# Spreading the decays' running sums with short products on four row groups of TensorE

## The chip, the cores and the metric

The kernel runs on one core of one Trainium2 chip, in one launch. The metric is the device time of an execution in microseconds (us); the runs are compared by their median.

## The reference, cut to what matters

The model is two stacked blocks over 256 tokens of width 1024, each of depth 2. The first block mixes three branches per layer: a state-space branch (ssd), latent attention, and a gated delta rule (gdn). The change concerns ssd and gdn, and there the decays. Both branches work in chunks and need, for every head, the difference of running sums of a decay `A` between every pair of positions of a chunk:

```
A_cum = jnp.cumsum(A, axis=-1)                                    # ssd: 16 heads
L = jnp.exp(jnp.where(tril, A_cum[..., :, None] - A_cum[..., None, :], -jnp.inf))
...
g = jnp.cumsum(chunks(g), axis=-1)                                # gdn: 8 heads
decay = jnp.exp(jnp.where(incl, g[..., :, None] - g[..., None, :], -jnp.inf))
```

On the chip a chunk is 128 positions for both branches (two chunks, c = 0 and 1), and position is the partition. So `A_cum[s]` down the partitions is a column, easily had, while `A_cum[t]` along the free axis has to be the same in all 128 partitions: a row that is spread to all partitions.

## The kernel before

**Engines and order.** Each engine runs its own program, written as generators; a hand-written order (`order1`) interleaves them turn by turn, the same order on every engine. A turn is either a step of a stage (gdn, ssd) or a "fill": one step of a large dense projection, 256 output columns, 48 matmuls in fp32r (lines 942 to 944, three per contraction tile, weights split in a high and a low half). ScalarE makes the high halves of the weights (line 1544), VectorE the low ones (line 2192; GpSimd for some), two chunks ahead. The weights come by 1 MB transfers into a ring of three units, each started by SyncE when TensorE is done with a unit.

**Banks.** PSUM has eight banks, and `open` hands them out strictly in turn: each call takes the oldest one and puts it at the end of the list (only the banks of a running power sum are held longer). TensorE waits in `open` until the previous user of that bank is emptied, that is, until the engines that read it have said so. So an `open` waits for the user that stands eight `open`s before it.

**The running sums.** `small` computes the decays `dA` [128 positions, 2 chunks, 24 heads] (0 to 15 ssd, 16 to 23 gdn) and by a product with the triangle `tri` the column form `cum` (lines 1085 to 1087, copied by ScalarE at 1807 and 1808). The row form is computed where it is needed, once per head and chunk: a column of `dA` broadcast to 128 columns is the stationary operand, `tri` the moving one, 128 rows of contraction (lines 1116 and 1247). All of these are fp32 products, and each shows as two records in the trace.

**gdn, four steps** `(c, g)` = (0,0), (0,1), (1,0), (1,1), each followed by a fill (`z`, `z`, `gate_g`, `gate_g`). TensorE opens bank `gd_b`, makes four row forms, opens `gd_qk` and makes four products of q and k (1122, 1123), then does the fill. ScalarE takes exp of `gd_b` (1836), waits for VectorE's clamp, takes exp of that (1839), makes high halves, and copies the fill's bank out through Silu or Sigmoid (1632), which is another table of functions. VectorE subtracts the column form from `gd_b` (2493), which empties it, clamps (2496), and makes the masked products (2498 to 2503). After the four steps come transposes (867) of what VectorE made.

**ssd, eight steps** `(c, q)`, four heads each: TensorE opens `sd_l` and makes four row forms; for the second chunk ScalarE takes exp of it (1925); VectorE subtracts and clamps (2627, 2631), which empties it, and ScalarE takes exp (1928). Fills stand behind six of the eight steps (`lat`, `lat`, none, `wgo`, `wgo`, `wgo`, none, `wgo`). `wgo` reads the gdn result, split by ScalarE (1579) and VectorE (2249). Then come the products of the stage (1256, 1269), the latter after VectorE's 2657.

Both layers of the first block run this; the second block does not use it.

Of the kernel before, what the change touches and what calls it, by code (L numbers as in the profile page):

```python
# [5 lines left out]
F32 = mybir.dt.float32  # L6
# [4 lines left out]
ACT = mybir.ActivationFunctionType  # L11
# [58 lines left out]
def bc(ap, shape):  # L70
    return ap.to_broadcast(shape)
# [89 lines left out]
class Shared:  # L161
# [18 lines left out]
    def up(self, who, name, tag):  # L180
        now = self.now
        assert not tag or (name, tag) not in now.after, (name, tag)
        assert now.owner.setdefault(name, who) == who, name
        now.n[name] = now.n.get(name, 0) + 1
        now.after[name, tag] = now.n[name]
        return self.sem(name), 1
# [4 lines left out]
    def at(self, name, tag):  # L191
        return self.sem(name), 1 if self.known is None else self.known.after[name, tag]
# [16 lines left out]
    def bank(self, tag):  # L209
        return self.ps[:, (self.known or self.now).bank_of[tag], :]  # L210
# [151 lines left out]
    def memory(self):  # L362
        nc = self.nc
        self.ps = self.ctx.enter_context(nc.psum_tensor("ps", [128, 8, 512], F32))
        self.home = (nc.sbuf_base + 31) // 32 * 32
        self.slab = self.sb("slab", [128, ARENA])
        self.ring = self.sb("ring", [128, (2 * RAW + HI) * SLOT])
        self.lows = [self.rounded(ARENA + 2 * i * SLOT, 2 * SLOT) for i in range(RAW)]
        self.highs = [self.rounded(ARENA + 2 * (RAW + i) * SLOT, 2 * SLOT) for i in range(HI // 2)]
        x2 = self.sb("x2", [128, 8, 512])  # L370
        self.x2 = x2[:, :, :]
        self.x = x2[:, :, 0:256]
        cst = self.sb("cst", [128, len(CONSTS), 128])
        self.cst = cst[:, :, :]
        self.C = {k: cst[:, i, :] for i, k in enumerate(CONSTS)}
        u = CONSTS.index("u0")
        self.upper = [cst[:, u + 2 * x:u + 2 * x + 2, :].rearrange("p n (a b) -> p (n a) b", b=16) for x in range(2)]
        o1, n1 = offsets(VEC1)
        o2, n2 = offsets(VEC2)
        v1, v2 = self.sb("v1", [128, 2, n1]), self.sb("v2", [128, 2, n2])  # L380
        self.v1, self.v2 = v1[:, :, :], v2[:, :, :]
        self.V1 = [{k: v1[:, l, a:b] for k, (a, b) in o1.items()} for l in range(2)]
        self.V2 = [{k: v2[:, l, a:b] for k, (a, b) in o2.items()} for l in range(2)]
        posi = self.sb("posi", [128, T], I32)
        trig = self.sb("trig", [128, 2 * T])
        self.posi, self.trig, self.cos, self.sin = posi[:, :], trig[:, :], trig[:, 0:T], trig[:, T:2 * T]
        qg8 = self.sb("qg8", [128, 1])
        self.qg8 = qg8[:, :]
        eps = self.sb("eps", [128, 1])
        self.eps = eps[:, :]  # L390
        zero = self.sb("zero", [128, 1])
        self.zero = zero[:, :]
        cvec, silc = self.sb("cvec", [128, 8, 2]), self.sb("silc", [128, 8, 50])
        self.cvec, self.silc = cvec[:, :, :], silc[:, :, :]
        row = self.sb("row", [128, 256])
        self.row = row[:, :]
        mods = self.sb("mods", [128, 2, 48, 2])
        self.mods = [mods[:, l, :, :] for l in range(2)]
        self.block1_memory()
        self.block2_memory()  # L400

# [448 lines left out]
class TensorE(Engine):  # L850
# [13 lines left out]
    def turn(self, P, aps):  # L864
# [2 lines left out]
            i = self.e.transpose(P[:, j * 128:j * 128 + 128], ap, self.K.C["ident"])  # L867
        return i

    def weights(self, chunk):  # L870

        K, p = self.K, self.K.take(chunk)
        if K.known is None:
            return p, K.lows[0][:, 0:K.wide_of(chunk)], K.lows[0][:, 0:K.wide_of(chunk)]
        if p in K.by_pool:
            self.wait_ge(*self.at("w_lo_g" if K.by_pool[p] else "w_lo_v", p))
            return p, K.high(p), K.low(p)
        self.wait_ge(K.raw_sem(p), K.raw_value(p))
        return p, K.raw(p), None
# [195 lines left out]
    def small(self, L):  # L1075
        K, up, at, e = self.K, self.up, self.at, self.e
        yield from self.rows(K.jobs1[L]["wsm"])
        yield
        yield
        yield  # L1080
        P = self.open("cum", L)
        self.wait_ge(K.sem("constants"), 16)
        self.wait_ge(*at("sm_v", "dA", L))
        dA = K.dA
        for c in range(2):
            self.mm(P[:, 24 * c:24 * c + 24], K.C["tri"], dA[:, c, :], True, True)
        self.mm(P[:, 64:88], K.C["ones"], dA[:, 0, :], True, True).then_inc(*up("sm_p", "cum", L))
        yield

    def qk(self, L):  # L1090
# [5 lines left out]
    def gdn(self, L):  # L1096
# [12 lines left out]
                self.turn(P, [vT[:, 4 * g + h, cs] for h in range(4)]).then_inc(*up("gd_p", "vt", L, c, g))  # L1109
        yield  # L1110

        for c, g in CG:
            cs = slice(c * 128, c * 128 + 128)
            P = self.open("gd_b", L, c, g)
            for j in range(4):
                i = mm(bank(P, j), bc(K.dA[:, c, 16 + 4 * g + j:17 + 4 * g + j], [128, 128]), K.C["tri"], True, True)
            i.then_inc(*up("gd_p", "b", L, c, g))
            P = self.open("gd_qk", L, c, g)
            self.wait_ge(*at("qk_v", "q", L))
            for j in range(2):  # L1120
                h = 2 * g + j
                mm(bank(P, 2 * j), kT[:, h, cs], kT[:, h, cs], True, True)
                i = mm(bank(P, 2 * j + 1), kT[:, h, cs], qT[:, h, cs], True, True)
            i.then_inc(*up("gd_p", "qk", L, c, g))
            yield
# [111 lines left out]
    def ssd(self, L):  # L1237
        K, up, at, e, mm = self.K, self.up, self.at, self.e, self.mm
        acc = K.s_acc

        yield

        for c in range(2):
            for q in range(4):
                P = self.open("sd_l", L, c, q)
                for j in range(4):
                    i = mm(P[:, j * 128:j * 128 + 128], bc(K.dA[:, c, 4 * q + j:4 * q + j + 1], [128, 128]), K.C["tri"], True, True)
                i.then_inc(*up("sd_p", "l", L, c, q))
                yield

        for c in range(2):
            cs = slice(c * 128, c * 128 + 128)
            P = self.open("sd_cb", L, c)
            self.wait_ge(*at("cv_s", "silu", ("xbc", L), 11))
            for g in range(2):
                i = mm(P[:, g * 128:g * 128 + 128], acc[:, 8 + g, cs], acc[:, 10 + g, cs], True, True)
            i.then_inc(*up("sd_p", "cb", L, c))
            for g in range(2):
                P = self.open("sd_x", L, c, g)
                self.turn(P, [acc[:, 4 * g + j, cs] for j in range(4)]).then_inc(*up("sd_p", "x", L, c, g))  # L1260
        yield

        P = self.open("sd_bt", L)
        self.turn(P, [acc[:, 8 + g, 0:128] for g in range(2)]).then_inc(*up("sd_p", "bt", L))
        for g in range(2):
            P = self.open("sd_h", L, g)
            self.wait_ge(*at("sd_v", "Xs", L))
            self.wait_ge(*at("sd_s", "bt", L))
            mm(P, K.Bt[:, g, :], K.Xs[:, 512 * g:512 * g + 512], True, True).then_inc(*up("sd_p", "h", L, g))
        yield  # L1270

        half = [slice(64 * j, 64 * j + 64) for j in range(2)]
        for c in range(2):
            for g in range(2):
                P = self.open("sd_y", L, c, g)
                self.wait_ge(*at("sd_v", "LC", L, c, 2 * g + 1))
                self.wait_ge(*at("sd_v", "Xd", L, c, g))
                for i in range(4):
                    for j in range(2):
                        h = 8 * g + 2 * i + j  # L1280
                        m = mm(P[half[j], 128 * i:128 * i + 128], K.Xd[:, c, 64 * h:64 * h + 64], K.L2[:, c, h, :], True, True)
                m.then_inc(*up("sd_p", "y", L, c, g))
            if c == 0:
                for g in range(2):
                    P = self.open("sd_off", L, g)
                    self.wait_ge(*at("sd_s", "h", L, g))
                    for i in range(4):
                        m = mm(P[:, 128 * i:128 * i + 128], K.Hs[:, g, 128 * i:128 * i + 128], acc[:, 10 + g, 128:256], True, True)
                    m.then_inc(*up("sd_p", "off", L, g))
            yield  # L1290

        self.stats(("so", L), 8, 4, T, K.C["ones"], K.sq)
        yield
# [237 lines left out]
class ScalarE(Engine):  # L1531
# [253 lines left out]
    def small(self, L):  # L1785
# [21 lines left out]
        self.act(K.cum, P[:, 0:48].rearrange("p (a b) -> p a b", a=2), ACT.Copy).then_inc(*up("sm_s", "cum", L))  # L1807
        self.act(K.tot, P[:, 64:88], ACT.Copy).then_inc(*up("sm_s", "tot", L))
        self.emptied("sm_s", "cum", L)
        yield  # L1810

    def qk(self, L):
# [1547 lines left out]
```

## Time and profile before

| | |
|---|---|
| median of 3 runs | 2505.55 us (2504.55 to 2507.82) |
| profiled execution | 2503.62 us, its span 2501.8 us |
| TensorE (PE) | busy 97% of the span, 20550 matmul records |
| VectorE (DVE) / ScalarE (ACT) / GpSimd (POOL) | busy 58% / 50% / 12% |
| mean granted TensorE clock | 0.988 of full |

The first block's layers lie at about 17 to 675 us and 675 to 1330 us; gdn's four steps run at 94 to 124 us and 753 to 783 us, ssd's eight at 258 to 301 us and 917 to 960 us. A row's start is counted from the span's start. Matmuls overlap, so the price of one in a stream is the distance between starts and not its duration. PE is TensorE's matmul, PEld its weight load, SP SyncE.

### The profile page before, as it was taken

To read this page: it belongs to the slowest core of one execution; us is meant where nothing else is said; L and a number is where in the kernel's file an instruction comes from. 1 tells how busy PE (TensorE), PEld (TensorE's weight loads), DVE (VectorE), ACT (ScalarE), POOL (GpSimd) and SP (SyncE) were. 2 spreads that over 40 slices of the span, in tenths; PEclk is the share of its full clock that TensorE was granted. 3 is DMA by queue.
4 is the path that set the end of the run, shared out by engine and by line. 5 is a ranking of instruction groups with operands and counts; after the bars stand their busy time and mean duration, and the time that the engine had idled before them with its cause. 6 is when DMAs were issued, how large, how long until landed. Compare 5 with 4: busy or idle time off the path is not lost.

```text
span 2501.8 us, 46658 instructions
## 1 busy us (share of the span) xinstructions
PE 2419.7 (97%) x20550; PEld 2251.4 (90%) x20550; DVE 1452.0 (58%) x2202; ACT 1244.5 (50%) x1832; POOL 301.2 (12%) x171
## 2 busy tenths in 40 slices
PE   6999999999999999999999999999999999998999
PEld 6999998999999999989999886887789997778999
DVE  5773776665457457756655347643335555776554
ACT  5745654554466375555544367532223444344442
POOL 4213000000141220001000004200000001331000
PEclk9999999999999999999999999999999999999999
DMA  4344444555444343545553235333325542213554
GB/s 174 136 151 169 149 160 164 196 183 192 157 169 152 138 167 135 186 163 193 188 189 129 101 136 202 127 115 130 104 99 198 199 145 99 86 69 135 185 186 169
DMA packets 56058, 383.01 MB, mean 153 GB/s; under 512 B 6064, under 2 KB 9776, under 8 KB 10288
## 3 DMA queue, kind: packets, MB, share of 16 engines
q1 hardware_dynamic: 55104, 375.90, 42.0%
q10 hardware_dynamic: 752, 4.13, 0.5%
q8 instruction: 162, 2.65, 0.4%
q14 instruction: 40, 0.33, 0.0%
HBM read 377.91 MB, written 1.05 MB: 151 GB/s over the span
## 4 chain that ended last, share of the span: by engine, by line
PE 80%; DVE 10%; ACT 6%; DMA 2%; issue 1%; POOL 0%; DVEq 0%; ACTq 0%; POOLq 0%
PE ps L942 20%; PE ps L944 20%; PE ps L943 20%; DVE r L2192 3%; ACT r L1544 2%; PE ps L1071 1%; PE ps L1023 1%; PE ps L1025 1%; PE ps L1024 1%; PE ps L980 1%; PE ps L901 1%; PE ps L981 1%; PE ps L982 1%; PE ps L867 1%; PE ps L1169 1%
## 5 line engine op out<-in xcount | busy, mean ns | idle before, releaser
L942 PE MATMUL ps<-r,r 128*128 128x256 f32 (+1 forms) x4464 | 1329.0, 298 | 8.7 <-DVE slab L2990 4.9
L943 PE MATMUL ps<-r,r 128*128 128x256 f32 (+1 forms) x4464 | 1314.1, 294 | 0.0
L944 PE MATMUL ps<-r,r 128*128 128x256 f32 (+1 forms) x4464 | 1313.2, 294 | 0.0
L2192 DVE TENSOR_TENSOR r<-ring,r 128x1024 fp32r<-128x1024 f32 (+2 forms) x558 | 678.0, 1249 | 515.8 <-ACT r L1544 515.5
L942 PEld LDWEIGHTS ps<-r,r 128*128 128x128 f32 x4464 | 843.8, 189 | 43.0 <-issue 5.8
L944 PEld LDWEIGHTS ps<-r,r 128*128 128x128 f32 x4464 | 843.2, 189 | 25.0
L943 PEld LDWEIGHTS ps<-r,r 128*128 128x128 f32 x4464 | 843.8, 189 | 24.2 <-issue 0.5
L1544 ACT ACTIVATE r<-ring 128x1024 fp32r<-128x1024 f32 (+1 forms) x614 | 612.7, 1038 | 280.4 <-DMA ring<-in_fo 63.7
L3114 POOL TENSOR_TENSOR slab<-slab 128x512 f32<-128x512 f32 (+1 forms) x20 | 28.7, 1433 | 1238.5 <-ACT slab L1660 1218.3
L3066 POOL TENSOR_TENSOR r<-ring,r 128x1024 fp32r<-128x1024 f32 x56 | 133.2, 2398 | 233.0 <-ACT r L1544 223.1
L2281 DVE SCALAR_TENSOR_TENSOR slab<-ps,v,slab 128x255 f32<-128x255 f32 (+1 forms) x168 | 67.8, 474 | 76.6 <-ACT slab L1612 76.6
L980 PE MATMUL ps<-r,r 128*128 128x256 f32 x288 | 86.9, 302 | 13.4 <-DVE r L2368 7.6
L1023 PE MATMUL ps<-r,r 128*128 128x256 f32 (+2 forms) x304 | 89.3, 294 | 0.4 <-DVE r L2192 0.4
L1025 PE MATMUL ps<-r,r 128*128 128x256 f32 (+2 forms) x304 | 87.4, 288 | 0.0
L1024 PE MATMUL ps<-r,r 128*128 128x256 f32 (+2 forms) x304 | 87.4, 287 | 0.0
L981 PE MATMUL ps<-r,r 128*128 128x256 f32 x288 | 84.3, 293 | 0.0
L982 PE MATMUL ps<-r,r 128*128 128x256 f32 x288 | 84.2, 292 | 0.0
L1681 ACT ACTIVATE r<-slab 128x512 fp32r<-128x512 f32 x33 | 20.8, 632 | 114.0 <-DVE slab L2350 114.0
L980 PEld LDWEIGHTS ps<-r,r 128*128 128x128 f32 x288 | 58.2, 202 | 16.9 <-DVE r L2368 9.1
L1632 ACT ACTIVATE slab<-ps 128x512 f32<-128x512 f32 x48 | 28.6, 595 | 80.1 <-PE ps L944 79.9
L3155 POOL TENSOR_TENSOR slab<-slab,posi 128x768 f32<-128x768 f32 (+1 forms) x24 | 38.6, 1609 | 226.2 <-DVE posi L2891 226.2
L1660 ACT ACTIVATE slab<-x 128x512 f32<-128x512 f32 x36 | 22.7, 631 | 78.0 <-DVE x L2326 45.7
(338 smaller groups left out, 2618.3 us busy)
## 6 DMA issues: line engine op xcount, KB each, us to landing
ring<-in_win SPq DMA_DIRECT2D x76, 1024.0 KB, 4.7
ring<-in_ada SPq DMA_DIRECT2D x48, 1024.0 KB, 4.9
ring<-in_fi SPq DMA_DIRECT2D x44, 1024.0 KB, 4.7
ring<-in_fo SPq DMA_DIRECT2D x36, 1024.0 KB, 4.8
ring<-in_wup SPq DMA_DIRECT2D x32, 1024.0 KB, 4.7
ring<-in_wdn SPq DMA_DIRECT2D x32, 1024.0 KB, 4.7
ring<-in_hin SPq DMA_DIRECT2D x20, 1024.0 KB, 4.7
ring<-in_nqkv SPq DMA_DIRECT2D x12, 1024.0 KB, 4.8
```

The source lines that it names most:

```text
L942: self.mm(o, hi[:, k - k0, cs], xh, k == 0, False)
L943: self.mm(o, hi[:, k - k0, cs], xl, False, False)
L944: i = self.mm(o, lo[:, k - k0, cs], xh, False, k == last)
L980: self.mm(o, hi, xh, k == 0 and t % per == 0, False, skip_group_check=True)
L981: self.mm(o, hi, xl, False, False, skip_group_check=True)
L982: i = self.mm(o, lo, xh, False, k == kt - 1, skip_group_check=True)
L1023: self.mm(o, xh, cut(hi, k), k == 0, False)
L1024: self.mm(o, xh, cut(lo, k), False, False)
L1025: i = self.mm(o, xl, cut(hi, k), False, k == kt - 1)
L1544: self.act(K.high(p), K.raw(p), ACT.Copy).then_inc(*self.up("w_hi", p))
L2192: self.tt(K.low(p), K.raw(p), K.high(p).bitcast(F32), ALU.subtract).then_inc(*self.up("w_lo_v", p))
L3066: self.tt(K.low(p), K.raw(p), K.high(p).bitcast(F32), ALU.subtract).then_inc(*self.up("w_lo_g", p))
```

## The change

Three things. `small` makes, after the column form, the row form once for all 24 heads: the stationary operand is `dA` [128, 24], the moving one `tri`, and the result [24 heads, 128 positions] is made four times per chunk, at partitions 0, 32, 64 and 96 of one bank (`cumT`). ScalarE copies that bank (256 columns) to memory that held the positions. Where a head's row form is needed, it is then a product with 24 rows of contraction: the stationary operand is a column of the identity broadcast to 128 columns, which picks the head, the moving one `cumT`. Four such products, one in each group of 32 partitions, stand next to each other and write four different banks. For that, gdn opens all four `gd_b` banks ahead of its first step, and ssd the four `sd_l` banks of a chunk ahead of that chunk's first step; what follows (q and k products, fills, the other engines' steps) keeps its order.

```
+        self.cumT = self.posi.bitcast(F32)
...
+    def row_of(self, q, h):
+        return bc(self.K.C["ident"][32 * q:32 * q + 24, 32 * q + h:32 * q + h + 1], [24, 128])
...
 TensorE.small
+        P = self.open("cumT", L)
+        for c in range(2):
+            for q in range(0, 128, 32):
+                i = self.mm(P[q:q + 24, 128 * c:128 * c + 128], dA[:, c, :], K.C["tri"], True, True)
+        i.then_inc(*up("sm_p", "cumT", L))
...
 TensorE.gdn
+        self.wait_ge(*at("sm_s", "cumT", L))
+        P = [self.open("gd_b", L, c, g) for c, g in CG]
+        for j in range(4):
+            for q, (c, g) in enumerate(CG):
+                i = mm(bank(P[q], j), self.row_of(q, 16 + 4 * g + j), K.cumT[32 * q:32 * q + 24, 128 * c:128 * c + 128], True, True)
+                if j == 3:
+                    i.then_inc(*up("gd_p", "b", L, c, g))
         for c, g in CG:
             cs = slice(c * 128, c * 128 + 128)
-            P = self.open("gd_b", L, c, g)
-            for j in range(4):
-                i = mm(bank(P, j), bc(K.dA[:, c, 16 + 4 * g + j:17 + 4 * g + j], [128, 128]), K.C["tri"], True, True)
-            i.then_inc(*up("gd_p", "b", L, c, g))
             P = self.open("gd_qk", L, c, g)
...
 TensorE.ssd
         for c in range(2):
-            for q in range(4):
-                P = self.open("sd_l", L, c, q)
-                for j in range(4):
-                    i = mm(P[:, j * 128:j * 128 + 128], bc(K.dA[:, c, 4 * q + j:4 * q + j + 1], [128, 128]), K.C["tri"], True, True)
-                i.then_inc(*up("sd_p", "l", L, c, q))
+            P = [self.open("sd_l", L, c, q) for q in range(4)]
+            for j in range(4):
+                for q in range(4):
+                    i = mm(P[q][:, j * 128:j * 128 + 128], self.row_of(q, 4 * q + j), K.cumT[32 * q:32 * q + 24, 128 * c:128 * c + 128], True, True)
+                    if j == 3:
+                        i.then_inc(*up("sd_p", "l", L, c, q))
+            for _ in range(4):
                 yield
...
 ScalarE.small
+        self.wait_ge(*at("sm_p", "cumT", L))
+        self.act(K.cumT, self.bank("cumT", L)[:, 0:256], ACT.Copy).then_inc(*up("sm_s", "cumT", L))
+        self.emptied("sm_s", "cumT", L)
```

## Rows read from the trace of the kernel before

**Rows 1.** The page: busy time by engine, and the chain that ended last.
```profile
PE 2419.7 (97%) x20550; PEld 2251.4 (90%) x20550; DVE 1452.0 (58%) x2202; ACT 1244.5 (50%) x1832; POOL 301.2 (12%) x171
...
PE 80%; DVE 10%; ACT 6%; DMA 2%; issue 1%; POOL 0%; DVEq 0%; ACTq 0%; POOLq 0%
```

**Rows 2.** Timeline of TensorE in gdn, layer 0: start, duration, operation.
```profile
94.17 1.06 PE L1116 MATMUL ps<-cst,slab 128*128 128x128 f32 x8
...
116.34 1.05 PE L1116 MATMUL ps<-cst,slab 128*128 128x128 f32 x8
117.22 0.39 PE L1122 MATMUL ps<-slab 128*128 128x128 f32 x2
...
118.04 0.36 PE L942 MATMUL ps<-r,r 128*128 128x256 f32 x1
```

**Rows 3.** Timeline of TensorE around 32-row products of the attention branch.
```profile
385.79 0.28 PE L1321 MATMUL ps<-slab 128*128 128x128 f32 x1
386.00 1.17 PE L1325 MATMUL ps<-x,slab 32*128 32x128 f32 x32
387.10 0.38 PE L942 MATMUL ps<-r,r 128*128 128x256 f32 x1
```

**Rows 4.** Timeline of TensorE around products on four column groups (256 columns).
```profile
228.09 1.07 PE L901 MATMUL ps<-ring,silc 128*32 128x256 f32 x16
229.09 0.38 PE L1227 MATMUL ps<-slab 128*128 128x128 f32 x1
```

**Rows 5.** Timeline of ScalarE in gdn, layer 0, third and fourth step.
```profile
112.18 0.60 ACT L1836 ACTIVATE slab<-ps 128x512 f32<-128x512 f32 x1
...
117.84 0.60 ACT L1632 ACTIVATE slab<-ps 128x512 f32<-128x512 f32 x1
118.46 1.28 ACT L1836 ACT_TABLE_LOAD   x1
119.75 0.60 ACT L1836 ACTIVATE slab<-ps 128x512 f32<-128x512 f32 x1
```

**Rows 6.** Timeline of VectorE, the fourth step of gdn, layer 0.
```profile
120.38 0.69 DVE L2493 TENSOR_TENSOR slab<-ps,slab 128x512 f32<-128x512 f32 x1 [1.08 <-ACT slab L1836]
```

**Rows 7.** Timeline of gdn, layer 1: its first VectorE step, the fourth fill, the fourth subtraction.
```profile
751.53 1.29 DVE L2478 TENSOR_TENSOR slab<-ps,slab 128x512 f32<-128x512 f32 x2 [0.48 <-PE ps L867]
...
776.94 0.36 PE L942 MATMUL ps<-r,r 128*128 128x256 f32 x1
...
779.01 0.69 DVE L2493 TENSOR_TENSOR slab<-ps,slab 128x512 f32<-128x512 f32 x1 [1.09 <-ACT slab L1836]
```

**Rows 8.** Timeline of ssd, layer 0: waits of TensorE and of VectorE.
```profile
266.41 0.36 PE L942 MATMUL ps<-r,r 128*128 128x256 f32 x1 [0.23 <-DVE r L2192]
...
274.37 0.36 PE L942 MATMUL ps<-r,r 128*128 128x256 f32 x1 [0.28 <-DVE r L2249]
...
288.74 0.69 DVE L2627 TENSOR_TENSOR slab<-ps,slab 128x512 f32<-128x512 f32 x1 [0.31 <-ACT slab L1925]
...
310.94 0.67 PE L1269 MATMUL ps<-slab 128*128 128x512 f32 x1 [1.59 <-DVE slab L2657]
```

**Rows 9.** Timeline of ssd, layer 1: the same around the first `wgo` fill.
```profile
930.85 0.60 ACT L1632 ACTIVATE x<-ps 128x512 f32<-128x512 f32 x1 [0.97 <-PE ps L944]
...
932.84 0.36 PE L942 MATMUL ps<-r,r 128*128 128x256 f32 x1 [0.24 <-DVE r L2249]
```

**Rows 10.** Waits of TensorE, whole span: total us, times, longest us.
```profile
PE ps L1335 <- DVE slab L2763: 8.6, 2, 4.5
```

**Rows 11.** Windows: us, PE busy (x), granted clock, DMA share, GB/s.
```profile
56.00:58.00 2.00, 0.00 (x0) 1.00 0.44 139
428.00:434.00 6.00, 6.00 (x31) 0.56 0.11 48
430.00:432.00 2.00, 2.00 (x11) 0.50 0.00 0
1087.00:1092.00 5.00, 5.00 (x25) 0.50 0.01 5
```

## The prediction

> **What bounds the kernel.** I read the page first: TensorE is busy 97% of the span and carries 80% of the chain that ended last [rows 1]. So by default a microsecond of TensorE is a microsecond of the kernel. But that is an average. Next I read TensorE's timeline through the stages that the diff touches, for what it waits for, then the timelines of ScalarE and VectorE beside it, for how far behind they run, and last the list of waits and the windows, for the clock.
>
> In gdn TensorE does not wait: from 94.17 to 116.34 us it does three steps, 7.39 us each [rows 2]. One step is the four row forms (116.34 to 117.22: 0.88 us), the q and k products (to 118.04: 0.82 us), and the rest, 5.69 us, the fill of 48 matmuls. ScalarE's step is longer: from 112.18 to 119.75 it is 7.57 us [rows 5]. It holds exp, a wait for VectorE's clamp, exp, two weight halves, a table load, the fill's copy, and a table load back (118.46, 1.28 us) before the next exp. So here two engines run at almost the same pace, and ScalarE is the slower one. The reader is to see that the fourth exp starts at 119.75, 3.4 us after TensorE began its operand, and VectorE's subtraction at 120.38 [rows 6]. The kernel gets away with it, since nobody waits for that bank soon.
>
> **The products that go.** Per layer 16 in gdn and 32 in ssd, in groups of four at 0.88 us [rows 2]: 24 groups in the two layers, 21.1 us of TensorE. **What replaces them** has a close analogue: the attention branch makes 16 products of 32 rows on four row groups into four banks, 32 records. They start at 386.00 and the next matmul at 387.10, 1.10 us, and 0.1 us more passes ahead of them (385.79 to 386.00) than between two ordinary records [rows 3]. I take 1.2 us for a burst of 16; 24 rows instead of 32 should not matter. The bounds are 1.1 us and, with no overlap at all, 3.5 us (four groups at 0.88). Six bursts: 7.2 us. **What is added**: per layer eight products on four column groups, 16 records of 128 columns. The row beside it has 16 records of 256 columns in 1.0 us [rows 4]; half the columns give 0.5 us, and I take 0.6 us, between 0.2 and 1.0. ScalarE's added copy of 256 columns is at most the 0.6 us of one of 512 [rows 5]. It stands behind the column form's copies, some 30 us ahead of gdn, in a stretch where TensorE has fills to do; late next are a weight half and some squares. I cost it at nothing, and at 0.4 us a layer if they are waited for.
>
> If TensorE's time were all, that would be 21.1 - 7.2 - 1.2 = 12.7 us off. It is not, and the reason is the banks.
>
> **gdn: the bank of the last row forms.** Write down the opens. Before: b0 qk0 fill0 b1 qk1 fill1 b2 qk2 fill2 b3 qk3 fill3. After: b0 b1 b2 b3 qk0 fill0 qk1 fill1 qk2 fill2 qk3 fill3. Banks come round every eight. Before, fill3 takes the bank of b1, emptied long ago. After, fill2 takes b1's, qk3 takes b2's, and fill3 takes b3's. b3 is emptied by VectorE's fourth subtraction, which needs ScalarE's fourth exp, which stands in ScalarE's order behind the copy of fill2 and a table load. In layer 0 that subtraction ends at 120.38 + 0.69 = 121.07 [rows 6]. Does that chain move? The copy of fill2 came at 117.84 [rows 5], 1.5 us after fill2's last matmul began ahead of 116.34 [rows 2]: it did not wait for TensorE, and operands made earlier don't speed it up. TensorE reaches fill3 earlier by 4 x 0.88 - 1.2 = 2.3 us, later by up to 0.6 us of `small`: at 115.7 to 116.3 instead of 118.04. Then it waits some 5 us, to 121.1. Fill3 starts 3.1 us later than before. In layer 1 the fourth subtraction ends at 779.70, and fill3 began at 776.94 [rows 7]: 2.8 us, and since there the chain hangs on TensorE's transposes (0.48 us of waiting for them at 751.53), `small`'s 0.6 us come on top: 3.4 us. Behind fill3 the transposes' results, the fills' copies and with them the weight halves are waited for from TensorE, so I see nothing that takes the loss back. gdn with `small`: +3.1 + 3.4 = +6.5 us.
>
> **The clock.** An idle stretch of 5 us is new in a stage that had none. TensorE waited for 2763 twice, 8.6 us together, the longer one 4.5 us, so the other 4.1 [rows 10]. Behind both the granted clock was down: from 428 to 434 us its mean is 0.56, which is 5.2 us at 0.50, the lower of the two levels (1.2 instead of 2.4 GHz), and 1087 to 1092 lies at 0.50 whole [rows 11]. In a wait that fills 56 to 58 us the clock stayed at 1.00 [rows 11]. At the low level there are 11 records in 2 us, where a fill has 48 in 5.69, or 17 in 2 us: 5.2 us of it cost 1.8 us, and counted by the halved clock 2.6 us. I take 2.0 us for each layer's wait: +4.0 us. The Trainium skill ("TensorE: Matmul & The Clock Gate", Why this matters for your kernels) warns against idle gaps between bursts for this reason. By that rule both new waits cost clock; the trace agrees for its two waits over 4 us.
>
> **ssd.** Banks: the fourth bank of the first chunk is taken again by the fill behind the second burst, long after VectorE is done with it; no wait. But TensorE's time does not come off in full. In layer 0, `lat`'s second fill starts at 266.41 for VectorE's weight half and the first `wgo` fill at 274.37 for VectorE's split [rows 8], so nothing is won up to there. Later VectorE no longer waits 0.31 us at 288.74 (for ScalarE, and that for the row forms), and the stage ends with TensorE waiting 1.59 us for VectorE's 2657, at 310.94 [rows 8], behind that chain: -0.3 us. In layer 1 ScalarE's copy at 930.85 waited 0.97 us for TensorE, which now comes 2 x 0.88 - 1.2 = 0.55 us earlier, and the split and the fill at 932.84 with it [rows 9]; with the same 0.3: -0.85 us. Bounds: 0, and TensorE's own shortening, 2 x (8 x 0.88 - 2 x 1.2) = 9.3 us. I take -1.15 us, near the lower end since the waits stand there.
>
> **The sum.** +6.5 + 4.0 - 1.15 = +9.35 us. Against the profiled execution (2503.62 us, span 2501.8, 1.8 us around it) that is 2513.0; the runs' median is 1.9 us above it, so 2505.55 + 9.35 = 2514.9 us.
>
> **Rivals.**
> (a) The wait comes, the clock stays up in one layer or both. For it: a wait of over 2 us left it alone [rows 11]. +7.35 us with one fall (2512.9), +5.35 with none (2510.9).
> (b) Faster: TensorE's time counts after all, since b3's bank is empty in time. This decides once ScalarE's fourth exp starts 4.8 us earlier than at 119.75, at 115.0 [rows 5]; for that its table loads (1.28 us) or the copy of fill2 would have to stand elsewhere. Then 2 x 2.3 and 1.15 are won, less 1.2 for `small`: -4.55 us, 2501.0; with all of ssd's 9.3 us -12.7, 2492.9. The Trainium skill ("TensorEngine Tiling (Array Packing)", Theoretical Speedup) states up to four times for 32 rows, the rule by which this change pays. The trace bears the factor out (16 products in 1.1 instead of 3.5 us), but in a place where no bank holds TensorE up.
> (c) Part of the loss is taken in by later waits of TensorE on work that does not hang on it. Against it: I found none. It would be within 5 us of 2505.55, say 2508.
> (d) The short products don't overlap (24 rows, a stationary operand from one column): a burst costs 3.5 us. In gdn that hides in the new wait, which shrinks to 2.7 us, and the clock stays up; in ssd two bursts a layer come in one piece, up to 1.7 us late for the fill behind the first. +6.5 + 2 x 1.7 = +9.9 us, 2515.5: the same side, another reason.
>
> **How the numbers follow.** The forecast with both falls 0.66, (a) 0.16, (b) 0.07, (c) 0.07, (d) 0.04. The time is the likeliest's, 2514.9. Its own spread: falls of 1.8 to 2.6 us (-0.4, +1.2), `small` with ScalarE's copy (-0.4, +1.2), ssd at 0 (+1.15), ssd at half of its bound (-3.5, rarely): 2511.5 to 2518.5. The range goes down for (a) and the upper half of (c): 2508.5 to 2518.5. 0.2% is 5.0 us, about what a measurement of this kernel can tell from no change. Slower: the forecast, (d), and (a) but for 0.03 of it below 5 us: 0.83. Same: that and most of (c): 0.10. Faster: 0.07.
>
> **What would show it.** The timeline after: a wait of about 5 us ahead of the second `gate_g` fill in each layer, released by VectorE's subtraction at about 121.1 in layer 0; the granted clock at 0.50 behind it for up to 5 us; bursts of 32 records on 24 rows with 1.1 to 1.2 us from their start to the next matmul; in `small` 16 records in 0.5 to 0.6 us; in ssd waits for 2192 and 2249 longer than before, and the stage shorter by 0.3 to 1 us. I am wrong if TensorE finds that bank free, or if the stages after gdn start no later than before.

## The result and the profile after

| | before | after |
|---|---|---|
| median | 2505.05 us (2504.17 to 2507.82, 4 runs) | 2519.40 us (2518.14 to 2520.01, 4 runs) |
| profiled span, us | 2501.8 | 2518.2 |
| mean granted TensorE clock | 0.988 | 0.983 |

The ratio is 1.0053, interval 1.0040 to 1.0066: the changed kernel is slower, by 14.35 us between the medians. The forecast was slower by 9.35 us, 2514.9 us. The time lies 0.9 us above the stated range. The direction came as forecast, and so did the mechanism in gdn; a third of the size is missing.

The page of the changed kernel, in the parts that answer to [rows 1], and the group of the dense fills' first matmul:

```profile
PE 2420.0 (96%) x20582; PEld 2247.4 (89%) x20582; DVE 1452.9 (58%) x2202; ACT 1245.5 (49%) x1834; POOL 302.1 (12%) x171
...
PE 78%; DVE 11%; ACT 7%; DMA 2%; issue 1%; POOL 0%; DVEq 0%; ACTq 0%; POOLq 0%
...
L947 PE MATMUL ps<-r,r 128*128 128x256 f32 (+1 forms) x4464 | 1334.0, 299 | 23.6 <-DVE slab L2511 9.4
```

TensorE is busy for as many microseconds as before, 2420, although the row forms now take a third of the time. That is the first thing to see: a busy microsecond at half clock counts as a microsecond, and the clock has eaten the saving (worked out behind the table below). The span grew by idle time, from 82 to 98 us of TensorE's, and 9.4 us of it stand in front of fills, for line 2511, which is line 2493 of before (lines moved by 5 to 18; 947 to 949 are 942 to 944). The list of TensorE's waits (total, times, longest):

```profile
PE ps L947 <- DVE slab L2511: 9.4, 2, 4.7
PE ps L1350 <- DVE slab L2781: 8.6, 2, 4.5
...
PE ps L1284 <- DVE slab L2675: 4.2, 2, 2.1
PE ps L947 <- DVE r L2267: 4.0, 2, 2.0
```

Line 1350's wait is [rows 10] unchanged. The first is new. The last two were 1.59 and 0.28 us long in layer 0 before [rows 8]. TensorE's timeline at the places that the forecast named, in order:

```profile
58.36 1.02 PE L1091 MATMUL ps<-slab,cst 128*128 128x24 f32 x4 [2.51 <-DVE slab L2468]
59.21 0.60 PE L1092 MATMUL ps<-slab,cst 128*128 128x24 f32 x2
59.74 1.07 PE L1096 MATMUL ps<-cst,slab 128*24 128x128 f32 x16
60.74 0.58 PE L947 MATMUL ps<-r,r 128*128 128x256 f32 x1
...
96.95 1.17 PE L1126 MATMUL ps<-posi,cst 24*128 24x128 f32 x32
98.05 0.49 PE L1135 MATMUL ps<-slab 128*128 128x128 f32 x2
...
123.51 0.58 PE L947 MATMUL ps<-r,r 128*128 128x256 f32 x1 [4.73 <-DVE slab L2511]
123.89 0.42 PE L948 MATMUL ps<-r,r 128*128 128x256 f32 x1
...
280.17 0.36 PE L947 MATMUL ps<-r,r 128*128 128x256 f32 x1 [2.02 <-DVE r L2267]
...
316.34 2.52 PE L1284 MATMUL ps<-slab 128*128 128x512 f32 x4 [2.08 <-DVE slab L2675]
...
726.00 0.64 PE L1096 MATMUL ps<-cst,slab 128*24 128x128 f32 x16
726.57 0.38 PE L947 MATMUL ps<-r,r 128*128 128x256 f32 x1
...
787.41 0.58 PE L947 MATMUL ps<-r,r 128*128 128x256 f32 x1 [4.67 <-DVE slab L2511]
```

The burst of sixteen short products takes 1.10 us to the next matmul (96.95 to 98.05). At 123.51 stands the new wait for b3's bank; in [rows 2] the same fill began at 118.04 without one. Who holds the bank is seen on ScalarE and VectorE, the fourth step, against [rows 5, 6]:

```profile
120.23 0.60 ACT L1647 ACTIVATE slab<-ps 128x512 f32<-128x512 f32 x1
120.84 1.28 ACT L1854 ACT_TABLE_LOAD   x1
122.14 0.60 ACT L1854 ACTIVATE slab<-ps 128x512 f32<-128x512 f32 x1
```
```profile
122.77 0.69 DVE L2511 TENSOR_TENSOR slab<-ps,slab 128x512 f32<-128x512 f32 x1 [1.09 <-ACT slab L1854]
```

It is the chain that the forecast drew: copy of the fill, table load, exp, subtraction, bank free at 123.46, fill at 123.51. Last the windows (us, TensorE busy and matmul records, granted clock, DMA share, GB/s):

```profile
59.00:61.00 2.00, 2.00 (x21) 0.50 0.48 201
61.00:64.00 3.00, 3.00 (x15) 0.50 0.01 3
...
123.00:126.00 3.00, 2.49 (x11) 0.51 0.00 0
...
317.00:320.00 3.00, 3.00 (x11) 0.60 0.40 169
...
787.00:790.00 3.00, 2.59 (x12) 0.50 0.01 3
...
945.00:948.00 3.00, 3.00 (x17) 0.61 0.70 287
...
982.00:986.00 4.00, 3.91 (x11) 0.65 0.46 195
```

At the same work the profile of before has a clock of 1.00 in all six places. Behind *every* wait of 2 us or more in the stages of the change, but the one at 280, TensorE ran at 1.2 instead of 2.4 GHz. The row of sums shows it best: the same sixteen records take 1.00 us at 59.74 and 0.57 us at 726.00.

**Where the 16 us of the profiled span went.** The start of the same work before and after, and the difference; each line's growth is what its stage cost:

| work | before | after | shift | grew by |
|---|---|---|---|---|
| layer 0: column sums (1091) | 58.85 | 58.36 | -0.49 | |
| gdn's first row forms | 94.17 | 96.95 | +2.78 | 3.27 |
| second `gate_g` fill | 118.04 | 123.51 | +5.47 | 2.69 |
| ssd's first row forms | 258.63 | 265.57 | +6.94 | 1.47 |
| ssd's products of 1284 | 310.94 | 316.34 | +5.40 | -1.54 |
| layer 1: column sums | 718.25 | 725.25 | +7.00 | 1.60 |
| gdn's first row forms | 753.08 | 760.84 | +7.76 | 0.76 |
| second `gate_g` fill | 776.94 | 787.41 | +10.47 | 2.71 |
| ssd's first row forms | 917.61 | 930.31 | +12.70 | 2.23 |
| ssd's products of 1284 | 969.41 | 982.09 | +12.68 | -0.02 |
| attention's transposes (1350) | 1051.49 | 1065.98 | +14.49 | 1.81 |

The last 1.9 us up to the end of the span (+16.4) come behind both layers. TensorE has the low clock there for about as long in both executions (25 us after, 26 us before), so the clock does not explain them, and their cause is not shown. The medians differ by 14.35.

Within the layers the clock does differ: read in windows of one microsecond, it is at the low level for 61 us after and for 34 us before, and the 27 us more are the stretches at 58, 123, 317, 787, 945 and 983. With the dense matmuls 213 ns apart there instead of 117, that is some 12 us by my estimate, about what the short products save (12.7 us by the forecast). What is left is the 16 us of idle time.

### The profile page after: what moved, and what is told of

Read it like the earlier page. It is cut to its first block, busy times and chain, and to the rows that moved or that the text cites. A ratio compares the mean times of both kernels' runs of the same rounds, so it can differ in the third digit from the quotient of the medians.

```text
span 2518.2 us, 46736 instructions
## 1 busy us (share of the span) xinstructions
PE 2420.0 (96%) x20582; PEld 2247.4 (89%) x20582; DVE 1452.9 (58%) x2202; ACT 1245.5 (49%) x1834; POOL 302.1 (12%) x171
## 4 chain that ended last, share of the span: by engine, by line
PE 78%; DVE 11%; ACT 7%; DMA 2%; issue 1%; POOL 0%; DVEq 0%; ACTq 0%; POOLq 0%
PE ps L947 20%; PE ps L949 20%; PE ps L948 20%; DVE r L2210 4%; ACT r L1559 2%; PE ps L1028 1%; PE ps L1030 1%; PE ps L1029 1%; PE ps L1076 1%; PE ps L985 1%; PE ps L906 1%; PE ps L987 1%; PE ps L986 1%; PE ps L1182 1%; DMA ring<-in_hin 1%
## 5 line engine op out<-in xcount | busy, mean ns | idle before, releaser
L3203 POOL TENSOR_TENSOR slab<-slab 128x512 f32<-128x512 f32 x32 | 49.9, 1561 | 94.8 <-PE ps L1481 52.3
```

## The experiments

Times are medians beside runs of the kernel before on the same chip; those had medians of 2504.78 (beside e1 to e4), 2505.03 (e5 to e8) and 2505.59 us (e9 to e12), each over 19 to 29 runs from 2501 to 2511. The ratio on record is not simply the quotient of the two medians (for e9 that would be 0.9992), so small differences are read from the ratios and their intervals. "Low stretches" are stretches in which TensorE had the low clock, read from windows of one microsecond over the whole span.

### e1: the order of the banks alone

The kernel before, with its 128-row products and no turned sums; only gdn's sixteen row forms stand ahead of the first step, in four banks.

```
+        P = [self.open("gd_b", L, c, g) for c, g in CG]
+        for j in range(4):
+            for q, (c, g) in enumerate(CG):
+                i = mm(bank(P[q], j), bc(K.dA[:, c, 16 + 4 * g + j:17 + 4 * g + j], [128, 128]), K.C["tri"], True, True)
```

> The old 128-row products from the decays, no cumT, ssd as before; only gdn's four banks are opened ahead of the first step. Bank theory: the wait for the fourth bank is there too, about 2.7 us long (the burst takes 3.55 us instead of 1.2, so TensorE arrives 2.4 us later), fill3 starts 3.1 and 2.8 us later than before, +5.9 us in all; a wait of 2.7 us may or may not lower the clock, up to +2 us a layer. Rival (the short products or the turned sums make the loss): no wait, within 0.5 us of before.

Measured: 2517.45 us (2515.62 to 2522.48, 5 runs), ratio 1.0053 (1.0040 to 1.0066), which is the whole loss of the change. TensorE's timeline, and ScalarE's in the second step of gdn:

```profile
125.04 0.58 PE L942 MATMUL ps<-r,r 128*128 128x256 f32 x1 [4.58 <-DVE slab L2495]
```
```profile
103.28 1.28 ACT L1634 ACT_TABLE_LOAD   x1
106.62 0.60 ACT L1634 ACTIVATE slab<-ps 128x512 f32<-128x512 f32 x1 [2.05 <-PE ps L944]
```

The order of the opens makes the wait without one short product. But the loss is 12.7 us, where at most 9.9 were expected, and the wait is 4.58 and not 2.7 us, not shorter by what the slower products take, since ScalarE's chain is not as free of TensorE as I had it: the copy of the first fill waits 2.05 us for that fill, which stands behind all sixteen products. A longer burst delays both sides of the race.

### e2, e3, e4: the parts one by one

e2 leaves ssd's row forms as before; e3 leaves gdn's as before; e4 computes and copies the turned sums, and nothing reads them.

```
-            P = [self.open("sd_l", L, c, q) for q in range(4)]
+            for q in range(4):
+                P = self.open("sd_l", L, c, q)
...
-        P = [self.open("gd_b", L, c, g) for c, g in CG]
+        for c, g in CG:
+            P = self.open("gd_b", L, c, g)
```

The first of these edits is e2's, the second e3's, and e4 has both; the 128-row products stand behind them as before.

> The change but for ssd, which keeps its old products. Bank theory: both 4.7 us waits and the low clock behind them stay, the fall of the clock behind ssd's wait for VectorE (line 2657 of before) goes: +6.5 for gdn with the sums, +4 for its clock, and what the clock costs in the sums' stretch: +10 to +13 us. Rival (ssd is the loss, by its clock falls): within 3 us of before.

> The change but for gdn, which keeps its old products in its old order. Bank theory: no wait in gdn; TensorE's work in ssd shrinks by 9.3 us, of which the profile of the changed kernel gives back about 2 us a layer before the clock falls behind the wait for VectorE: between -3 and +3 us of before, by how often the clock falls. Rival (each part costs alike): +5 us.

> The turned sums are computed and copied, and nobody reads them: both stages keep their old products. By the forecast +0.6 us a layer, +1.2 us in all. If the fall of the clock at 58 us that the changed kernel shows belongs to the sums, it is here too, +3 us more; if it is a matter of when the windows of the chip fall, it may be absent.

| | median, us | runs | ratio and interval |
|---|---|---|---|
| e2 gdn only | 2518.24 | 6 (2512.58 to 2522.11) | 1.0054 (1.0040 to 1.0067) |
| e3 ssd only | 2510.81 | 7 (2507.14 to 2514.03) | 1.0026 (1.0015 to 1.0037) |
| e4 sums only | 2508.03 | 11 (2502.47 to 2513.57) | 1.0014 (1.0005 to 1.0024) |

e2 has the two waits of 4.73 us and the changed kernel's time: 13.5 us lost, 10 to 13 expected. e3 has neither, and still loses 6.0 us: its expectation of 3 us at most was missed, and the rival's 5 is nearer. Its timeline shows what became of ssd's shorter products:

```profile
274.41 0.35 PE L947 MATMUL ps<-r,r 128*128 128x256 f32 x1 [2.03 <-DVE r L2264]
...
310.57 1.87 PE L1281 MATMUL ps<-slab 128*128 128x512 f32 x3 [2.08 <-DVE slab L2672]
```

TensorE comes to ssd's first row forms 1.18 us later than before (259.81 against 258.63), and yet the first `wgo` fill starts at 274.41, where it started at 274.37 [rows 8]. So the shorter products take that lateness in, and the rest of what they save is a wait of 2.03 us in place of 0.28. At 310.57 TensorE is 0.37 us early and has waited 0.49 us longer. Most of the saving is not on the path, as forecast. But behind the longer waits come low stretches that before did not have, at 311 and 936 us. e4 costs 3 us, within what it was expected to (1.2, and up to 3 more for a fall of the clock). The difference between e3 and e4, 2.8 us for ssd's part, is one that their intervals leave open. The turned sums of one layer take 0.57 us at full clock; e4's profiled execution (2511.63, above its median) also has a low stretch at 57 us behind a wait of 2.75 us. e1 has that one at 58 too, without any turned sums, and before waited 2.92 us there with the clock at 1.00. So the sums are not needed for this fall. It comes in some executions and not in others, and how much of e4's median is due to it is not shown.

### e5: two bursts of eight

The changed kernel; gdn opens b0 b1, takes two steps, opens b2 b3, takes the other two. Now the last fill comes round to the bank of the first fill.

```
+            if n % 2 == 0:
+                pair = list(enumerate(CG))[n:n + 2]
+                P = [self.open("gd_b", L, c2, g2) for q, (c2, g2) in pair]
```

> The changed kernel, but gdn fills its banks in two bursts of eight products on two row groups each (two banks, two steps, two banks, two steps), so that the second slab fill after the last step takes the bank of the first one's fill and no longer one that VectorE must empty. Theory (the order of the banks makes gdn's loss): both waits of 4.7 us for line 2511's subtraction are gone and with them the low clock behind them; the ssd part and the sums stay as in the kernel with only those (2510.8), and gdn's products give back 1.8 to 2.4 us a layer: 2505 to 2509 us. Rival (the row-group products themselves or the wait for the turned sums cost it): the time stays near the changed kernel's, 2516 to 2520. A burst of eight on two groups takes 0.55 us if two groups overlap as well as four, 0.9 if only two products run at once.

Measured: 2505.05 us (2502.93 to 2509.20, 11 runs), ratio 1.0000 (0.9992 to 1.0009). Both waits are gone, the second `gate_g` fill starts at 118.88 with no idle time, and the whole loss with them. TensorE's timeline of the second burst:

```profile
110.39 1.16 PE L1131 MATMUL ps<-posi,cst 24*128 24x128 f32 x16
111.48 0.49 PE L1138 MATMUL ps<-slab 128*128 128x128 f32 x2
```

Eight products on two row groups take 1.09 us, as long as sixteen on four: missed by the expectation on both its bounds. They still beat two steps' 128-row forms, 1.76 us.

### e6: exponentials and subtractions ahead

The changed kernel; since all four banks are full at once, ScalarE takes the four exponentials in a row, VectorE the four subtractions and clamps, ScalarE the four exponentials of those. Only the masked products stay in their steps.

```
             self.emptied("gd_s", "gd_b", L, c, g)
+        for c, g in CG:
+            s4 = slice(8 * c + 4 * g, 8 * c + 4 * g + 4)
             self.wait_ge(*at("gd_v", "D", L, c, g))
...
+        for _ in range(4):
             yield
```

This is ScalarE's part; VectorE's loop is split in the same way.

> The changed kernel, but ScalarE takes all four exponentials of the sums, VectorE all four subtractions and clamps, and ScalarE then the four exponentials of the differences, in gdn's first step, since all four banks are full by then; the later steps keep only the masked products. Theory: the four banks are empty about 10 us before the fill that wants the last of them, both gdn waits are gone (or a new shorter one of 1 to 3 us stands where the longer first step holds VectorE's or ScalarE's part of a weight chunk up); 2504 to 2510 us. Rival: the long first step delays the convolution's or the dense job's part on both engines, so that TensorE waits 4 us or more at another line and the time stays at 2515 or above.

Measured: 2505.84 us (2501.21 to 2515.16, 12 runs), ratio 1.0006 (0.9996 to 1.0016). ScalarE's timeline in layer 0:

```profile
98.12 2.04 ACT L1854 ACTIVATE slab<-ps 128x512 f32<-128x512 f32 x4
...
104.59 1.28 ACT L1647 ACT_TABLE_LOAD   x1
...
115.44 0.60 ACT L1647 ACTIVATE slab<-ps 128x512 f32<-128x512 f32 x1 [2.70 <-PE ps L949]
...
121.94 0.60 ACT L1647 ACTIVATE slab<-ps 128x512 f32<-128x512 f32 x1 [4.00 <-PE ps L949]
```

The banks are empty by 103.4 instead of 123.5, and now ScalarE waits for TensorE. From gdn's row forms (94.56) to the transposes behind its steps (121.75) it is 27.19 us, where before took 29.56. Here the short products pay what the forecast's TensorE-only sum said of gdn, 2.4 us a layer. The median does not show it: ssd's waits and low stretches are still there (272 and 965 us).

### e7, e8: the same waits, but not idle

e7 is the changed kernel with twenty repeated products of keys by keys in gdn's last step, in a bank that the real ones then overwrite. e8 adds nine products of the identity by the triangle ahead of layer 0's column sums and eight ahead of line 1284's products.

```
+            if (c, g) == CG[3]:
+                for n in range(20):
+                    mm(bank(P, n % 4), kT[:, n % 4, cs], kT[:, n % 4, cs], True, True)
```

> The changed kernel with twenty repeated 128-column products of keys by keys (4.3 us, into the bank that the real ones then overwrite) ahead of gdn's last step, so that TensorE works through most of the 4.7 us in which it would wait for line 2511. The fill behind them starts when it did before. Theory (the wait costs its own length and the low clock behind it costs extra): no low clock at about 123 and 787 us, time 3 to 5 us shorter than the changed kernel's 2519.4: 2514 to 2517. Rival (the low clock is not due to the idle wait, or costs nothing that counts): 2518 to 2521.

> As the one with busy products in gdn, and also nine repeated products ahead of layer 0's running sums (where TensorE waits 2.5 us for dA) and eight ahead of ssd's product of line 1284 (2.1 us), in both layers: the same waits, but TensorE is never idle in them. Theory (the low clock behind these waits makes the part of the loss that the waits themselves do not): the low stretches at 58, 123, 317, 787 and 983 us are gone and the time falls to 2508 to 2513 us, with waits as long as in the changed kernel. Rival (the waits alone make the loss): 2517 to 2521.

Measured: e7 2515.96 us (2512.09 to 2518.19, 5 runs), ratio 1.0041 (1.0029 to 1.0053); e8 2509.10 us (2506.47 to 2514.03, 11 runs), ratio 1.0016 (1.0007 to 1.0024). TensorE's timeline of e7, and two windows of e7 behind the waits' ends:

```profile
117.64 4.62 PE L1135 MATMUL ps<-slab 128*128 128x128 f32 x40
...
123.37 0.38 PE L947 MATMUL ps<-r,r 128*128 128x256 f32 x1 [0.21 <-DVE slab L2514]
```
```profile
122.00:125.00 3.00, 2.79 (x24) 1.00 0.02 5
...
788.00:791.00 3.00, 3.00 (x28) 1.00 0.03 8
```

TensorE is idle for 0.21 us here and for up to 0.96 us (the column sums) in e8. The fill starts when it did in the changed kernel, 123.37 against 123.51, and finds a clock of 1.00 and not 0.51. Between the medians the clock behind the two waits is worth 3.4 us; the intervals of e7 and of the change overlap, so that size is rough. Behind all five filled ones it is 10.3 us, clear of both intervals: of the 14 us lost, some 10 are clock (one of these five stretches, behind the column sums, may fall to the kernel before as well: e1 and e9 have it with no turned sums). e8 still stands 4.1 us above before: the waits, filled as they are, keep their length. The Trainium skill ("TensorE: Matmul & The Clock Gate", Why this matters for your kernels) advises against long idle gaps of TensorE between bursts of matmuls. The two runs agree, and put 10 us on it; but three of the five waits are shorter than the gaps the page has in view (2.1 to 2.5 us), and the low clock stood behind them too.

### e9: the new order with the old products

As e6, with 128-row products, no turned sums, and ssd as before.

```
-                i = mm(bank(P[q], j), self.row_of(q, 16 + 4 * g + j), K.cumT[32 * q:32 * q + 24, ...], True, True)
+                i = mm(bank(P[q], j), bc(K.dA[:, c, 16 + 4 * g + j:17 + 4 * g + j], [128, 128]), K.C["tri"], True, True)
```

> The kernel before, with gdn's four banks opened ahead and filled by the old 128-row products, and with the exponentials and subtractions moved ahead as in the kernel at 2505.8; no turned sums, ssd as before. Theory: without the wait, the order alone costs nothing, so this stands where the kernel before stands or a little under (fewer table loads on ScalarE, nothing taken from TensorE): 2502 to 2507 us; the whole rewrite of the products (row groups in gdn and ssd, sums turned) is then worth the difference between 2505.8 and this, between -3 and +3 us. Rival (the row-group products gave much, and moving the exponentials cost as much): 2509 or more.

Measured: 2503.48 us (2501.46 to 2508.74, 11 runs), ratio 0.9997 (0.9987 to 1.0006). With the short products and the turned sums added, that is e6, at 2505.84: 2.4 us more, which the two intervals leave open. In layer 0 the way from gdn's row forms (94.22) to the transposes (123.78) is 29.56 us, to the hundredth that of before. So the 2.4 us a layer of e6 are the short products', and the order by itself costs nothing once the exponentials stand ahead.

### e10: the products of a bank in a row

The changed kernel with its two loops exchanged, in gdn and in ssd, so that four products in a row use one row group.

```
-        for j in range(4):
-            for q, (c, g) in enumerate(CG):
+        for q, (c, g) in enumerate(CG):
+            for j in range(4):
```

> The changed kernel with the products of each bank in a row, four on the same row group one after the other, in gdn and ssd, in place of side by side. Each sixteen then take about 3.4 us in place of 1.1. Theory: what the overlap gives is taken back by waits whose end other engines set (gdn's for line 2511, ssd's two of about 2 and 1.4 us), so the time rises little: 2518 to 2523 us, and gdn's wait shrinks from 4.7 to 2.5 us or so. Rival (the overlap is on the path that sets the end): six bursts at 2.3 us each, 2531 to 2535.

Measured: 2527.95 us (2521.26 to 2529.91, 5 runs), ratio 1.0087 (1.0073 to 1.0101). Neither expectation met it. TensorE's timeline:

```profile
94.39 2.81 PE L1126 MATMUL ps<-posi,cst 24*128 24x128 f32 x32
97.13 0.49 PE L1135 MATMUL ps<-slab 128*128 128x128 f32 x2
...
122.43 0.52 PE L947 MATMUL ps<-r,r 128*128 128x256 f32 x1 [4.59 <-DVE slab L2511]
```

Sixteen take 2.74 us instead of 1.10. The wait did not shrink, for e1's reason: ScalarE's first copy waits 1.48 us for a fill that comes later. Six bursts of 1.64 us are 9.8 us, and the medians are 8.6 apart. The profiled execution was the shortest of the five (2521.26), so its rows explain less of the median than elsewhere.

### e11, e12: the best that these parts give

e11 is e6 with the repeated products of e8 ahead of layer 0's column sums and of line 1284. e12 adds eighteen in attention, meant for the wait of line 1350.

```
+            if (i, hp) == (1, 0):
+                for n in range(18):
+                    mm(P[:, 0:128], K.C["ident"], K.C["tri"], True, True)
```

> The kernel with the exponentials and subtractions ahead (2505.8), and the repeated products ahead of layer 0's running sums and ahead of ssd's product of line 1284, so that TensorE isn't idle there. Theory (waits of 2 to 3 us bring the low clock behind them, work in them keeps it high): 3 to 5 us less, 2500 to 2504 us, under both kernels; low clock at 965 us gone. Rival: unchanged, 2505 to 2508.

> As the one before, and eighteen repeated products (3.8 us) in attention's wait of 4.1 to 4.5 us ahead of the transposes of the probabilities (line 1350), in both layers, where both kernels have the low clock for 6.8 us. Theory: another 3 us a layer less, 2494 to 2498 us. Rival (the low clock there comes from the light work around the wait, or the repeated products hold up TensorE's next work): 2500 or more.

Measured: e11 2500.04 us (2495.78 to 2503.81, 12 runs), ratio 0.9981 (0.9973 to 0.9990): the fastest kernel here, 5.6 us under before. Its windows behind line 1284 in layer 1:

```profile
963.00:966.00 3.00, 2.75 (x13) 1.00 0.83 330
966.00:969.00 3.00, 3.00 (x28) 1.00 0.00 0
```

e6 has 7 records at 0.50 in that second window. The profiled execution of e11 is its fastest, 2495.78. e12 rose to 2508.31 us (2503.00 to 2512.50, 12 runs), ratio 1.0012 (1.0003 to 1.0020). The products stand in the wrong bank. TensorE's timeline:

```profile
413.06 4.18 PE L1354 MATMUL ps<-cst 128*128 128x128 f32 x36
417.07 0.60 PE L1359 MATMUL ps<-cst,slab 128*128 128x128 f32 x4
...
425.20 1.09 PE L1359 MATMUL ps<-cst,slab 128*128 128x128 f32 x4 [3.05 <-DVE slab L2795]
```

They stand two turns ahead of the wait, where TensorE had work, and only push the rest back, by some 4 us in each layer; the wait behind them is still 3.05 us. e12 says nothing of the clock. Whether repeated products in the kernel before, without any of the change, would gain as much as e11 was not tried.

## Why the prediction was right, and what it mis-sized

**The bank of the last row forms: right.** TensorE waits 4.73 and 4.67 us for it (forecast some 5), released by the fourth subtraction through the chain that was named. e1 shows that the order of the opens is enough to make the loss, e5 and e6 that undoing either side of it, the order or the late exponentials, takes it away. The second `gate_g` fill with all of `small` was to be 3.1 and 3.4 us late; it was 5.47 us in layer 0, and in layer 1 3.47 us (10.47 less 7.00).

**That ScalarE's chain does not move with TensorE in layer 0: wrong, and worth 2.4 us.** The fourth exp slid from 119.75 to 122.14 when gdn began 2.78 us later. I read the copy of the third fill, which indeed waits for nothing, and took the chain for free as a whole. But its first copy is tied to the first fill (e1, e10), and gdn's first exp to the transposes ahead of the steps: it slid by the same 2.39 us (98.12 to 100.51), behind VectorE's first step, which now waits 0.50 us for TensorE's transposes. Had the chain stayed, as the sum had it, the fill would have started at 121.1 whatever happened earlier; the 5.47 us above are 3.1 and this slide.

**`small`: its price right, its place wrong.** Sixteen records in 0.5 to 0.6 us were forecast and are 0.57 us in layer 1. In layer 0 a low stretch stands behind the wait ahead of them, and gdn starts 3.27 us later against its column sums' start. I had cited that very wait, 56 to 58 us at a clock of 1.00 [rows 11], as evidence that a wait of this length leaves the clock alone. It was one execution's luck: of the eleven kernels profiled in which this wait was idle (2.1 to 3.1 us), eight have the low clock behind it, before and two others have not; the three in which it was filled have none.

**The clock behind gdn's waits: right.** 2.0 us a layer were taken; 1.47 and 2.23 us stand in the table, and e7 gives 3.4 us for both, roughly.

**ssd: the step that failed.** The burst of 1.10 us was right, and so was layer 1's way from the row forms to the first `wgo` fill, 0.63 us shorter (0.55 forecast). "Nothing is won up to there" in layer 0 was wrong by 1.14 us (15.74 us before, 14.60 after): TensorE came to the stage 6.94 us late, but VectorE, for which it waits there, only 5.60 (259.99 to 265.59), and the wait took in most of the difference. So -1.54 us in layer 0 was more than the -0.3. But the sum ended there; it put the clock behind ssd's waits at nothing. A TensorE that saves time ahead of a fixed wait waits longer, and a longer wait can cost clock behind it: +1.60 us in layer 0, and +1.79 us in layer 1 (-0.02 +1.81), where another low stretch at 945 lies within ssd. Forecast -1.15 us for both layers, measured +1.9: this and the slid chain in layer 0, which `small`'s low stretch set off, are the missing 5 us. By the terms: `small` and the wait 8.9 (forecast 6.5), clock behind it 3.7 (4.0), ssd 1.9 (-1.15), together 14.5 (9.35).

**The rivals.** (a), the clock stays up, did not come: behind gdn's waits of 4.6 to 4.7 us it was low in every profile that has them idle, eight waits of eight. (b), faster, fails on its own condition: the fourth exp did not start at 115.0. With the exponentials ahead (e6) its condition is met, and still the time is that of before: gdn's gain is there, and ssd's waits and low stretches take it. (c) came for about 1 us, in layer 0's wait for the first `wgo` fill; the rest of the loss is kept, 14.49 us at the last row of the table. (d), no overlap, fell by the 1.10 us; e10 shows what it would have cost, with the price of a burst at 2.74 and not 3.5 us.

**Left open.** Which execution gets a low stretch behind a given 2 us wait, and which does not. How much of e11's gain belongs to the change. And what the last 1.9 us of the profiled span are.

## What to carry to other kernels

Where buffers are handed out in turn, moving an `open` ahead changes who waits for whom eight opens later: write both sequences down before counting what the work itself saves. Time taken from an engine ahead of a wait for another engine is not gained; it makes the wait longer, and on TensorE a longer wait can also slow what comes behind it. A busy time that has not moved does not say that nothing was saved: look at the clock beside it. A clock that stayed up behind a short wait in one profile is one draw, and belongs in the range as a cost, not in the sum as nothing.

## What the runs showed of the hardware

- A burst of products on row groups, from its start to the next matmul: sixteen of 24 rows on four groups 1.10 us, eight on two groups 1.09 us, sixteen on four groups but four in a row on each 2.74 us, and four of 128 rows 0.88 us [rows 2]. Halving the groups doubles the time per product, and short products on one group still came a little faster (0.17 us each) than those of 128 rows (0.22). The Trainium skill ("TensorE: Matmul & The Clock Gate", Why this matters for your kernels) states that one product of 32 rows takes as long as one of 128 and that all the gain lies in their running side by side; the runs agree in the main, 2.5 times between 2.74 and 1.10 us.
- The low clock is a matter of chance behind waits of about 2 us. Behind ssd's wait for line 1284 (or its like), idle for 1.6 us (the wait of before), none of ten had it; idle for 2.1 us, 8 of 12; filled with products, none of six. The wait for the first `wgo` fill, idle for 2.02 us, had it behind 5 of 18, so the length does not decide alone. Behind gdn's waits of 4.6 to 4.7 us it was 8 of 8 idle and none of four filled. One fall cost 1.4 to 1.6 us where 3.4 us ran low, with the dense matmuls 213 ns apart instead of 117.
